# Conditioning sums move from GpSimd and TensorE to VectorE, and the second attention's scores contract over 96 partitions

## What is computed

```
cond = silu(c)                                   # (1, 1024)
for i in range(2):
    mod = cond @ ada_w[i] + ada_b[i]             # (1024) @ (1024, 6144): six segments of 1024
    sh_m, sc_m, g_m, sh_f, sc_f, g_f = split(mod, 6)
    hm = rms(x, norm_mix[i]) * (1 + sc_m) + sh_m
    x = x + g_m * mixer_i(hm)
    hf = rms(x, norm_ffn[i]) * (1 + sc_f) + sh_f
    x = x + g_f * ((silu(a) * b) @ ffn_w_out[i]),  a, b = split(hf @ ffn_w_in[i])
```

## Time and profile before

| | before |
|---|---|
| median of 3 runs | 774.35 us |
| the profiled execution | 771.15 us |
| its span on the core | 769.4 us |
| TensorE busy | 708.3 us, 92% |
| VectorE busy | 522.0 us, 68% |
| ScalarE busy | 374.7 us, 49% |
| GpSimd busy | 274.7 us, 36% |

### The profile page before, as it was taken

The page is one execution under the profiler, slowest core; times in us unless marked ns, Lnnn a source line. Parts: engine busy times, 40 slices in busy tenths (PEclk is TensorE's granted clock), DMA queues, the critical chain, the costliest instruction groups (busy, mean ns, idle before and its releaser), DMA issues. The chain is left out here.

```text
span 769.4 us, 10825 instructions
## 1 busy us (share of the span) xinstructions
PE 708.3 (92%) x3889; PEld 568.7 (74%) x3889; DVE 522.0 (68%) x940; ACT 374.7 (49%) x696; POOL 274.7 (36%) x261
## 2 busy tenths in 40 slices
PE   4799998989968999989999699989969999999997
PEld 2576768778647888868888486868648888878886
DVE  3357687898466887676766877987567885554544
ACT  3255555676336544433433367776346444444431
POOL 7021211000103997979979432520106960000000
PEclk9999998999988999999999999999989999999999
DMA  8997993030653888884877455801845965555521
GB/s 289 357 375 218 351 374 110 1 111 2 206 177 111 270 270 268 276 277 155 289 268 232 131 171 175 296 31 56 279 159 171 287 207 182 172 179 196 168 106 55
DMA packets 93741, 154.03 MB, mean 200 GB/s; under 512 B 6235, under 2 KB 68320, under 8 KB 93696
## 3 DMA queue, kind: packets, MB, share of 16 engines
q1 hardware_dynamic: 80768, 111.24, 44.1%
q0 software_dynamic: 12928, 42.20, 16.5%
HBM read 151.32 MB, written 1.05 MB: 198 GB/s over the span
## 5 line engine op out<-in xcount | busy, mean ns | idle before, releaser
L1077 DVE TENSOR_TENSOR w_lo<-raw,w_hi 128x1024 fp32r<-128x1024 f32 (+3 forms) x198 | 289.8, 1480 | 138.6 <-ACT w_hi L732 138.1
L732 ACT ACTIVATE w_hi<-raw 128x1024 fp32r<-128x1024 f32 (+3 forms) x198 | 201.7, 1026 | 273.4 <-PE lin L1724 249.7
L1722 PE MATMUL lin<-w_hi,st_hi 128*128 128x512 f32 (+2 forms) x568 | 229.7, 404 | 0.1
L1724 PE MATMUL lin<-w_hi,st_lo 128*128 128x512 f32 (+2 forms) x568 | 220.8, 389 | 0.0
L1723 PE MATMUL lin<-w_lo,st_hi 128*128 128x512 f32 (+2 forms) x568 | 220.5, 388 | 0.0
L600 POOL DMA_DIRECT2D ada_ring<-in_ada_w_dram x80 | 45.4, 568 | 259.3 <-PE sc L1835 222.2
L1722 PEld LDWEIGHTS lin<-w_hi,st_hi 128*128 128x128 f32 x568 | 108.9, 192 | 29.3 <-issue 7.9
L1724 PEld LDWEIGHTS lin<-w_hi,st_lo 128*128 128x128 f32 x568 | 108.5, 191 | 21.7
L1723 PEld LDWEIGHTS lin<-w_lo,st_hi 128*128 128x128 f32 x568 | 108.9, 192 | 19.0 <-issue 0.5
L679 POOL TENSOR_TENSOR pool_acc<-pool_acc,ada_ring 128x1024 f32<-128x1024 f32 x40 | 110.8, 2770 | 3.3
L678 POOL TENSOR_SCALAR ada_ring<-ada_ring,cond_b 128x1024 f32<-128x1024 f32 x40 | 65.5, 1639 | 20.4 <-DMA pool_acc<-in_ada_b_dram 18.7
(11 more groups left out here) (258 smaller groups left out, 870.5 us busy)
## 6 DMA issues: line engine op xcount, KB each, us to landing
raw<-in_ffn_w_in_dram SPq DMA_DIRECT2D x88, 512.0 KB, 4.9
ada_ring<-in_ada_w_dram POOLq DMA_DIRECT2D x80, 512.0 KB, 5.0
raw<-in_ffn_w_out_dram SPq DMA_DIRECT2D x22, 1024.0 KB, 5.0
raw<-in_nsa_w_in_dram SPq DMA_DIRECT2D x10, 1024.0 KB, 12.6
ada_first<-in_ada_w_dram SPq DMA_DIRECT2D x8, 1024.0 KB, 13.0
raw<-in_nsa_cmp_w_dram SPq DMA_DIRECT2D x4, 1024.0 KB, 9.6
raw<-in_nsa_w_out_dram SPq DMA_DIRECT2D x4, 1024.0 KB, 9.6
raw<-in_mla_w_out_dram SPq DMA_DIRECT2D x4, 1024.0 KB, 7.9
```

Of the source, the lines that this page charges most:

```text
L732: nc.scalar.activation(part_of(w_hi, s), raw_part(s), ACT.Copy).then_inc(hi_ready, 1)
L1077: nc.vector.tensor_tensor(part_of(w_lo, s), raw_part(s), part_of(w_hi, s).bitcast(F32), ALU.subtract).then_inc(lo_ready, 1)
L1722: nc.tensor.matmul(bank, a_h, w_h, start=first, stop=False)
L1724: return nc.tensor.matmul(bank, a_l, w_h, start=False, stop=last)
```

## The change

`VEC_SEGS` = 2, 5, 6, 7, 8, 9, 10, 11 are summed by VectorE: one `scalar_tensor_tensor` of 128 x 1024 a chunk (multiply by `cond`, add to `acc`), 64 in all. GpSimd clears the accumulator, issues the bias and the chunks, and waits for VectorE's sum before it issues chunk a+3. TensorE keeps 3 and 4; all eight others end in `reduce_row` or `reduce_columns`. The reduces are spread: 5 before unit 9, 6 before unit 10, 7, 8, 9 in DOWN0 after k = 8, 11, 14, 10 and 2 as `row_done`. The pads are not cleared, and the scores read `[0:DQ]`, 96 partitions.

The core of the diff:

```diff
-POOL_SEGS = (5, 6, 7, 8, 11)
+VEC_SEGS = (2, 5, 6, 7, 8, 9, 10, 11)
             def issue_next(a):
                 if a + ARING < NSEG * KD:
-                    if seg_at(a // KD) not in POOL_SEGS:
+                    if seg_at(a // KD) in VEC_SEGS:
+                        pool.wait_ge(acc_summed, chunks_by_dve(a + 1))
+                    else:
                         pool.wait_ge(ada_used, chunks_by_pe(a + 1))
                     issue(a + ARING)
+            def prepare(seg):
+                n = VEC_SEGS.index(seg)
+                layer, s6 = divmod(seg, 6)
+                link(nc.gpsimd.memset(acc[:, n % 4, :], 0.0))
+                if n > 0:
+                    pool.wait_ge(acc_bias, 16 * n)
+                pool.dma_start(acc[0:1, n % 4, :],
+                               ada_b[layer:layer + 1, s6 * D:(s6 + 1) * D]).then_inc(acc_bias, 16)
+            pool.wait_ge(slot_used, OUT0)
+            prepare(2)
+            prepare(5)
+            supply(2)
...
-            link(nc.gpsimd.memset(q1_t[DQ:P], 0.0))
-            nc.gpsimd.memset(k1_t[DQ:P], 0.0).then_inc(pads_zero, 1)
...
+            pool.wait_ge(scored, 3 * H)
+            prepare(10)
             supply(10)
+            prepare(11)
+            supply(11)
```

```diff
+            def ada_sum(count=1):
+                for _ in range(count):
...
+                    if kt == 0:
+                        dve.wait_ge(acc_bias, 16 * (m + 1))
+                    else:
+                        dve.wait_ge(acc_summed, KD * m + kt)
+                    dve.wait_ge(ada_landed[n % ARING], 16 * (n // ARING + 1))
+                    nc.vector.scalar_tensor_tensor(total, ada_ring[:, n % ARING, :], cond_b[:, kt, 0:1], total,
+                                                   ALU.mult, ALU.add).then_inc(acc_summed, 1)
...
+                if t == 0:
+                    ada_sum()
+                if n in (22, 27):
+                    ada_sum()
             output_low(T_O0)
-            low_to(OUT0 + 8)
+            for last, n in ((5, 2), (6, 2), (7, 1), (8, 0)):
+                low_to(OUT0 + last)
+                ada_sum(n)
...
+                        if q < sums_in(u):
+                            ada_sum()
+            for n in range(5 * KD - 3 * FU):
+                low_to(DOWN0 + 6 + n)
+                ada_sum()
...
             output_low(T_O1)
-            low_to(OUT1 + 8)
+            for last, n in ((5, 2), (6, 3), (7, 3), (8, 0)):
+                low_to(OUT1 + last)
+                ada_sum(n)
```

```diff
-            for _ in range(ARING):
-                ada_chunk()
-            unit(U_OUT1, OUT1, FOUR, 512, stationary, st_wait(T_O1, o_batch(o1)), EACH)
-            last_unit(U_OUT1 + 1, OUT1 + 4, lambda: ada_turned(10))
+            unit(U_OUT1, OUT1, FOUR, 512, stationary, st_wait(T_O1, o_batch(o1)))
+            last_unit(U_OUT1 + 1, OUT1 + 4, lambda: reduce_columns(10))
...
-            reduce_row(8)
-            unit(U_IN1 + 1, INB1, FOUR, QL, stationary, key_value_latent, (2, 3))
+            unit(U_IN1 + 1, INB1, FOUR, QL, stationary, key_value_latent)
...
-                      lambda n, t: q1_t[:, n, t * P:(t + 1) * P],
-                      lambda n, tiles: k1_t[:, n, 0:tiles * P],
+                      lambda n, t: q1_t[0:DQ, n, t * P:(t + 1) * P],
+                      lambda n, tiles: k1_t[0:DQ, n, 0:tiles * P],
```

More of the change, by code:

```diff
@@ L165, in rows_by_pe, with chunks_by_dve @@
 def rows_by_pe(seg):
-    return sum(s not in POOL_SEGS for s in ADA_ORDER[:ADA_ORDER.index(seg)])
+    return sum(s not in VEC_SEGS for s in ADA_ORDER[:ADA_ORDER.index(seg)])
 def chunks_by_pe(a):
-    return sum(seg_at(n // KD) not in POOL_SEGS for n in range(EARLY * KD, a))
+    return sum(seg_at(n // KD) not in VEC_SEGS for n in range(EARLY * KD, a))
+def chunks_by_dve(a):
+    return sum(seg_at(n // KD) in VEC_SEGS for n in range(EARLY * KD, a))
 def stationary_number(batch):
@@ L1252, in feed_forward @@
                 silu0 = counts["silu"]
-                for u in range(3):
+                for u in range(FU):
+                    in_unit(u)
                     unit(u)
[L1255 to L1261, removed]
                 counts["silu"] = silu0 + T * FU
@@ L1857, in ada_chunk @@
                 next_chunk[0] += 1
[L1858 removed]
+                while next_chunk[0] < NSEG * KD and seg_at(next_chunk[0] // KD) in VEC_SEGS:
                     next_chunk[0] += KD
@@ L1867, in ada_turned @@
                 ins.then_inc(ada_red, 1)
[L1869 to L1877, removed]
             def wait_acc(seg):
-                pe.wait_ge(acc_pool, POOL_SEGS.index(seg) + 1)
+                pe.wait_ge(acc_summed, KD * (VEC_SEGS.index(seg) + 1))
                 pe.wait_ge(ada_out, ada_at(seg) - 1)
@@ L1984, in feed_forward @@
                     one(4, i)
-                at_end()
-                one(FU - 2)
-                one(FU - 1)
+                for u in (FU - 2, FU - 1):
+                    in_unit(u)
+                    one(u)
                 def down_product(k, ns, tiles=range(T)):
@@ L2239, in _, with next_mods, mixer_mods @@
                 o_batch(o0)(T_O0, m)
-            unit(U_OUT0, OUT0, FOUR, 512, stationary, st_wait(T_O0, o_batch(o0)), EACH)
-            last_unit(U_OUT0 + 1, OUT0 + 4, lambda: ada_spread(2))
+            unit(U_OUT0, OUT0, FOUR, 512, stationary, st_wait(T_O0, o_batch(o0)))
+            last_unit(U_OUT0 + 1, OUT0 + 4, lambda: reduce_row(2))
             for m in range(2):
                 x_batch(T_HF0, m)
-            def next_mods():
-                reduce_row(5)
-                reduce_columns(6)
-            def mixer_mods():
-                reduce_columns(7)
-            feed_forward(UP0, DOWN0, U_UP0, T_HID0, T_HF0, at_end=next_mods, in_down=mixer_mods)
+            def next_mods(u):
+                if u == FU - 2:
+                    reduce_row(5)
+                else:
+                    reduce_columns(6)
+            def mixer_mods(k):
+                if k == 8:
+                    reduce_columns(7)
+                elif k == 11:
+                    reduce_row(8)
+                elif k == 14:
+                    reduce_columns(9)
+            feed_forward(UP0, DOWN0, U_UP0, T_HID0, T_HF0, next_mods, mixer_mods)
             for m in range(2):
@@ L2278, in _ @@
                     latent_transposes(2)
-                unit(U_KVB1 + u, KVB1 + u, [[3, 4]], 512, stationary, None, (0,))
+                unit(U_KVB1 + u, KVB1 + u, [[3, 4]], 512, stationary)
             def key_transposes(first, last):
@@ L2297, in _ @@
             for u in range(2):
-                unit(U_QB1 + u, QB1 + 2 * u, [[0, 1], [2]], QU, stationary, None, (0,))
+                unit(U_QB1 + u, QB1 + 2 * u, [[0, 1], [2]], QU, stationary)
             for u in range(2, 4):
```

134 lines of the change are left out of this document (61 added, 73 removed).

## The result

| | before | after |
|---|---|---|
| median of the runs (4 each, interleaved) | 774.39 us | 784.29 us (781.3 to 786.6) |
| ratio, 95% interval | | 1.0123 (1.0083 to 1.0164) |
| span of the profiled execution | 769.4 us | 779.4 us |
| first transposes of OUT0 | 193.40 | 195.83 |
| first transposes of UP0 | 231.56 | 231.36 |

The differences of neighbouring rows say where the 10.0 us of the span come from: +2.43, -2.63, -2.84, -6.48, then **+10.65 in the second attention**, +8.22 in OUT1, and +0.65 from UP1 to the end. The forecast for these was +1.9, -3.3, -2.6, -7.5, **0**, +7.3, 0. Six of the seven are within 1.1 us; the one that was put at nothing decides the sign.

The account below looks back on a forecast made before the run. The prediction took TensorE, busy for 92% of the span, to bound the kernel. Its terms, 0.4 + 1.0 + 0.5 - 3.3 - 6.0 + 3.4 - 7.5 + 7.3 = -4.2, moved the median from 774.35 to 770.1 us, range 762.5 to 776.

Parts of the forecast that it names:

- Second attention, "0": Second attention: contraction over 96 partitions costs 0, from weight loads over 64 and 128 partitions taking 186 and 192 ns.
- rival on the contraction: Second attention: 96 partitions cost or save something, 0.4 us either way, time 770; chance 0.02.
- OUT1, +7.3: OUT1: TensorE waits 6.2 us for segment 10's eight sums, then slow reduce and steps, less removed work: +7.3 (+4.0 to +9.7).
- the term for the stop ahead of OUT0: Ahead of OUT0: TensorE's idle time grows to 2.3 us from 0.79, clock may fall: +0.5 (0 to 2.8, with OUT1).
- UP0 and its end, DOWN0, -6.0 + 3.4 = -2.6: UP0's sums hidden, 0; its end without stop at full clock, -6.0; DOWN0 takes in two reduces, +3.4.
- the two slower rivals: Chunks late in UP0 and UP1: 788 us, chance 0.07; sums longer than 1.68 us in UP0: about 792 us, 0.05.
- Behind IN1, -7.5: Behind IN1 to second attention: a reduce, pad clearing with its stop, slow stretch and chunks go: -7.5 (-10.9 to -5.5).
- To OUT0, +1.9: Start to OUT0: accumulator clearing +0.4, two sums at items 22 and 27 +1.0, longer idle ahead of OUT0 +0.5.
- OUT0, -3.3: OUT0: five chunks leave TensorE at 0.66 us each: -3.3 (-3.8 to -1.0).

Follow-up runs that it names:

- e1_before_96: The kernel before with one edit, the second attention's scores contract over 96 partitions (pads still cleared); 786.72 us, ratio to before 1.0184.
- e2_after_128: The changed kernel with scores over 128 partitions again and GpSimd clearing the pads behind segment 9's issues; 773.49 us, ratio to before 1.0005.
- e3_after_ten_early: The changed kernel (96 partitions) with segment 10 summed in DOWN0, none of its sums in OUT1; 774.81 us, ratio to before 1.0016.
- e4: The changed kernel with scores over 128 partitions, pads cleared, and segment 10 summed in DOWN0; 764.12 us, ratio to before 0.9860.
- g4_fillers: e4 with idle 128 x 128 products on TensorE in five places where it stands still; 754.04 us, ratio to before 0.9738.

## Why the prediction was wrong, step by step

- **Second attention, "0": this step failed.** It rested on the durations of weight loads over 64 and 128 partitions, and these were right. But a duration at full clock says nothing of the clock. The earlier trace rows showed a stop of 1.51 us that the clock survived; I used it for the stop ahead of OUT0, by its length alone, and did not ask whether this stop would still be survived once the change made the products beside it narrow. In the runs it was survived only behind full scores of head 8. Price: +10.65 us in the changed kernel, +14 by itself in `e1_before_96`; without it the time is 773.49 (`e2_after_128`), within the range. The rival on the contraction was priced by weight loads, 0.4 us, with a chance of 0.02; the mechanism by which it could hurt wasn't among the rivals at all.
- **OUT1, +7.3 (measured +8.22): right, with some luck.** The wait is 7.13 us (6.2 forecast), the eighth sum ends at 565.5 against 564.0, the reduce runs at the lower clock and takes 3.43. `e3_after_ten_early` shows that it was the sums' place and not their work. The luck: the sum took the second attention at full clock, and with that (`e2_after_128`) OUT1 lost its clock at its start as well and cost +11.64, outside +4.0 to +9.7, though the term for the stop ahead of OUT0 held up to 2.8 us for such a fall here too.
- **UP0 and its end, DOWN0, -6.0 + 3.4 = -2.6 (measured -2.84): right.** The reduces of 5 and 6 cost no stop. The sum's 1.28 us and the landings in UP0 (median 5.8, at most 7.8 us) leave nothing of the two slower rivals that I had priced. In DOWN0 VectorE does wait for three chunks, 3.4 us in all; no wait of TensorE stands in the trace there.
- **Behind IN1, -7.5 (measured -6.48): right in kind, 1 us too much.** The stop of 2.73 us is gone, the `tensor_scalar` on 128 x 4 takes 0.17 us in place of 3.53. VectorE sets the pace in KVB1 and QB1 as said, and TensorE now shows the wait for it, 1.43 us in one place:

```profile
478.88 0.44 PE L1762 MATMUL lin<-w_hi,st_hi 128*128 128x384 f32 x1 [1.43 <-DVE w_lo L1085]
```

- **To OUT0, +1.9 (measured +2.43): not to be told from the spread.** 1.1 us of that lie ahead of the change's first edit: a landing that TensorE waits for at 100 us, 1.35 in place of 0.50 us. This part of the code is the same in both; over the fourteen profiles its end lies between 125.3 and 129.0 us. Between there and OUT0 the kernels with before's code take 65.1 us in four profiles and 67.5 to 68.7 in five, and only in the five, before among them, is the clock low around 130 to 138 us; the changed kernel takes 69.0. The idle time ahead of OUT0 grew from 0.79 to 2.23 us (2.3 forecast). The clock falls behind it, and the second transposes with the six steps behind them take 3.19 us in place of 1.85: 1.3 us, where 0.5 was put.
- **OUT0, -3.3 (measured -2.63): right in kind.** That slow stretch lies in this stage. In e2, e3 and e4, where it is longer, the stage gives -1.5 to -0.8.
- **The range** ended at 776. Its bound for the second attention was a duration, so no part of it could hold 10 us more.

Open: why the scores over 64 partitions in the first attention don't bring its clock down from 142 us on, where it is 1.00 in the kernel before. Its stops are shorter there (up to 0.8 us, where this one is 1.51), and a group of eight such products takes 0.93 us where four over 128 take 0.82, so two may run at a time on both halves of the array; neither was tried.

## What to carry to other kernels

Rows of the array that are left empty cost no time in a product at full clock (four scores take 0.87 us over 96 and over 128 partitions), but just ahead of a stop of TensorE they may cost its clock: read the granted clock of the stage, not only the product's duration, and keep the contraction at the full 128 rows where that is free. Where work is taken off TensorE, ask which idle time it used to fill; the steps behind the longer stop can lose clock, and idle products can buy it back. A single profile is one draw for such a fall: compare several executions, or kernels that share the stage. Chunks that come through a ring of three are better summed one a slot over many slots than eight in a row just ahead of the one who waits.

## What was not expected of the hardware

- A narrow product of one head (96 of 128 rows) just ahead of a stop of 1.51 us lets the granted clock fall to 0.50 (six profiles of six, and once more with 112 rows); the same stop behind a full product doesn't (six of six), with seven narrow heads behind it or eight ahead.
- Uninterrupted work did not bring the clock back while narrow products went on, 24 us in the changed kernel; with only full products behind the same stop it took one slow head (518.07 to 521.27). In `e1_before_96` the clock was still low 10 us behind the start of the last narrow scores (541.13 to some 552).
- The idle products of `g4_fillers` in five stops took some 7 to 10 us off a kernel of 764.
